# Three transformer-like blocks on one core: stage ends as written sequences, a first tile in halves, warmed matmuls, a reordered mixer

## The reference

```
# first network, layer 0 (norms 1 and 2) and layer 1 (norms 3 and 4)
x = layer_norm(alpha * x + diff_attention(x, w_qkv, ...) @ w_o)         # norm 1
x = layer_norm(alpha * x + (silu(x @ gate) * (x @ up)) @ ffn_w_out[0])  # norm 2
x = layer_norm(alpha * x + chunk_attention(x, k_band, v_band, ...) @ b_w_o)  # norm 3
x = layer_norm(alpha * x + swiglu(x, ffn_w_in[1], ffn_w_out[1]))        # norm 4
# second network
z = rmsnorm(x, pre_mix_g) @ w_in                  # splits into zu, zv, zq, zk, zv2, zg, zlr
mixed = concat(gmlp_mixer(zu, zv), gla_mixer(zq, zk, zv2, zg, zlr)) @ w_out
x = x + rmsnorm(mixed, post_mix_g)                                      # norm 5
f = relu(rmsnorm(x, pre_ff_g) @ w_ff1) ** 2 @ w_ff2
out = x + rmsnorm(f, post_ff_g)                                         # last norm
```

## Time and profile before

| | |
|---|---|
| median of 3 runs | 1797.64 us (1797.47 to 1800.77) |
| the profiled execution | 1800.18 us, span 1797.3 us |
| TensorE matmul busy | 1769.7 us (98%), 8602 instructions |
| VectorE busy | 878.4 us (49%) |
| ScalarE busy | 673.6 us (37%) |
| POOL busy | 13.1 us (1%) |
| mean granted TensorE clock | 0.996 |
| HBM read | 173.32 MB |

### The profile page before, as it was taken

The page is one execution under the profiler, slowest core; times in us unless marked ns, Lnnn a source line. Parts: engine busy times, 40 slices in busy tenths (PEclk is TensorE's granted clock), DMA queues, the critical chain, the costliest instruction groups (busy, mean ns, idle before and its releaser), DMA issues.

```text
span 1797.3 us, 21277 instructions
## 1 busy us (share of the span) xinstructions
PE 1769.7 (98%) x8602; PEld 1448.5 (81%) x8602; DVE 878.4 (49%) x1435; ACT 673.6 (37%) x1125; POOL 13.1 (1%) x39
## 2 busy tenths in 40 slices
PE   8999999999999999999999999999999999999998
PEld 6777778888888897667888888888878898888886
DVE  4688773433333634555733333339436762434353
ACT  4467623222223234655222231233444542324141
POOL 0000000000000000000000000000000000000000
PEclk9999999999999999999999999999999999999999
DMA  8232223323333343222233332353223323233321
GB/s 279 93 98 85 86 81 105 107 82 102 98 94 118 94 129 93 72 83 77 71 100 97 102 117 71 95 152 107 60 60 103 108 94 105 87 102 94 106 82 47
DMA packets 218019, 176.84 MB, mean 98 GB/s; under 512 B 8977, under 2 KB 177842, under 8 KB 217922
## 3 DMA queue, kind: packets, MB, share of 16 engines
q1 hardware_dynamic: 217922, 175.49, 32.5%
HBM read 173.32 MB, written 7.38 MB: 101 GB/s over the span
## 4 chain that ended last, share of the span: by engine, by line
PE 95%; DVE 3%; ACT 1%; issue 0%; DMA 0%; SPq 0%; ACTq 0%
PE ps L559 29%; PE ps L561 29%; PE ps L560 28%; PE ps L817 2%; PE ps L859 1%; PE ps L883 1%; PE ps L871 1%; PE ps L837 1%; PE ps L756 1%; PE ps L827 0%; DVE wlo L1314 0%; PE ps L847 0%; DVE x L1403 0%; DVE arena L1443 0%; DVE small L1407 0%
## 5 line engine op out<-in xcount | busy, mean ns | idle before, releaser
L559 PE MATMUL ps<-xh,whi 128*128 128x512 f32 (+1 forms) x1184 | 443.9, 375 | 0.2 <-DVE xl L1327 0.2
L561 PE MATMUL ps<-xh,wlo 128*128 128x512 f32 (+1 forms) x1184 | 432.6, 365 | 0.0
L560 PE MATMUL ps<-xl,whi 128*128 128x512 f32 (+1 forms) x1184 | 432.0, 365 | 0.0
L1314 DVE TENSOR_TENSOR wlo<-raw,whi 128x1024 fp32r<-128x1024 f32 x235 | 283.2, 1224 | 251.4 <-ACT whi L1018 250.7
L1018 ACT ACTIVATE whi<-raw 128x1024 fp32r<-128x1024 f32 x235 | 243.6, 1050 | 125.4 <-PE ps L561 85.0
L559 PEld LDWEIGHTS ps<-xh,whi 128*128 128x128 f32 x1184 | 223.4, 189 | 45.8 <-issue 10.5
L559 PE MATMUL ps<-whi,hh 128*128 128x512 f32 x640 | 255.1, 399 | 3.7 <-DVE hl L1540 3.7
L561 PEld LDWEIGHTS ps<-xh,wlo 128*128 128x128 f32 x1184 | 223.3, 189 | 36.4
L560 PEld LDWEIGHTS ps<-xl,whi 128*128 128x128 f32 x1184 | 223.6, 189 | 35.9 <-issue 1.4
L561 PE MATMUL ps<-whi,hl 128*128 128x512 f32 x640 | 250.4, 391 | 0.0
L560 PE MATMUL ps<-wlo,hh 128*128 128x512 f32 x640 | 250.2, 391 | 0.0
(11 more groups left out here) (197 smaller groups left out, 2026.3 us busy)
## 6 DMA issues: line engine op xcount, KB each, us to landing
raw<-in_ffn_w_in SPq DMA_DIRECT2D x88, 512.0 KB, 4.0
raw<-in_w_ff SPq DMA_DIRECT2D x64, 512.0 KB, 4.2
raw<-in_ffn_w_out SPq DMA_DIRECT2D x44, 512.0 KB, 3.8
raw<-in_a_w_qkv SPq DMA_DIRECT2D x24, 512.0 KB, 4.8
raw<-in_w_in SPq DMA_DIRECT2D x20, 512.0 KB, 3.8
raw<-in_kv_w SPq DMA_DIRECT2D x16, 512.0 KB, 4.3
bias_skewed<-bias_rows SPq DMA_DIRECT2D x8, 640.0 KB
raw<-in_a_w_o SPq DMA_DIRECT2D x8, 512.0 KB, 4.7
```

Of the source, the lines that this page charges most:

```text
L559: e.matmul(o, ah, bh, start=start, stop=False)
L560: e.matmul(o, ah, bl, start=False, stop=False)
L561: return e.matmul(o, al, bh, start=False, stop=stop)
L1314: e.tensor_tensor(lo, self.raw[:, m % RAW, :], f32(hi), ALU.subtract).then_inc(s.lo, 1)
```

## The change

It has six parts.

- Each stage end (norms 1 to 5) is a written list of words, `EDGES`. L is the next left piece in order, a0 to a3 the last left piece of a row block, b0 to b3 the next right piece of a row block. T loads the root's function table, p is one pump, n, y, f, x are `ln`, `yscale`, `feat`, `xsplit` of a row block. Behind the bar, h is the first half of the next projection, and F ends the list. Between the first word that isn't a piece and F only p pumps.
- At norm 1 the early pieces are 19 instead of 15. At norm 3 they stay 15. At norm 5 five pieces instead of three stand ahead of the squares.
- The first tile of the kernel and its blocks of x are transferred, split and multiplied in two halves each. Ahead of them TensorE does 16 matmuls of 128x128 ones, whose result nobody reads.
- In the last norm the weights are multiplied in ahead of the root, the left halves between other row blocks and the right halves beside the squares. Then one operation scales by the root and adds to x. POOL's adds go.
- The mixer's string has another order.
- The explicit table load ahead of each head's Ln goes.

```
-ORDER_MIX = "v4 C0 C1 v4 D0 v4 T0 I0 D1 v4 T1 U0 I1 g4 U1 g4 O0 g4 N0 N1 O1 g4 N2 N3 z z6 V z10"
+ORDER_MIX = "v4 C0 C1 v4 D0 v3 D1 v1 T0 I0 v3 g1 T1 v1 I1 g2 U0 g1 U1 g4 O0 g2 N0 g1 N1 g1 O1 g1 N2 g1 N3 g2 z z6 V z10"
+EDGES = {
+    1: """L L L L L L L L L L L L b0 b0 p p b0 b1 b2 b1 p b1 a0 b0 a1 b2 T p b1 n0 a2 b2 n1 b3 b2 f0 x0 a3 n2 b3
+        f1 x1 b3 p b3 f2 | x2 h n3 h h f3 F p x3 h""",
+    2: """L L L L L L L L L L L L a0 a1 a2 a3 b0 b0 b0 T p b0 n0 b1 b1 b1 b1 n1 b2 f0 x0 b2 b2 b2 b3 f1 x1 n2 b3
+        b3 b3 | h f2 x2 n3 h h f3 x3 p p h F""",
+    3: """L L L L L L L L L L L L b0 b0 b0 a0 a1 a2 a3 T p b0 n0 b1 b1 b1 b1 n1 b2 f0 x0 b2 b2 b2 b3 f1 x1 n2 b3
+        b3 b3 | h f2 x2 n3 h h f3 x3 p p h F""",
+    4: """L L L L L L L L L L L L a0 a2 b0 b0 T a1 b0 p p b0 a3 n0 b1 b1 b1 b1 y0 n1 b2 b2 b2 b2 f0 x0 b3 b3 b3 y1
+        f1 p x1 n2 b3 | h y2 n3 p y3 h f2 x2 h h f3 h x3 F""",
+    5: """L L L L L L L L b0 b0 L L L L a0 a1 a2 p p b0 b0 T n0 b1 a3 b1 b1 b1 y0 n1 b3 b2 b2 b2 b2 b3 f0 y1 b3 x0
+        f1 x1 n2 p b3 | h y2 n3 h h p f2 p y3 x2 h h f3 F x3 h""",
+}
...
             if t == 3:
                 self.done(tile, "rows", r.value)
-            if ends and first and t == 3 and norm >= 4:
-                self.feat(norm, 0)
-                self.xsplit(norm, 0)
-            elif ends and first and t >= 2 and norm < 4:
-                self.feat(norm, t - 2)
-                self.xsplit(norm, t - 2)
...
-            for _ in range(15):
+            for _ in range(ready_pieces(1)):
                 next(out)
...
-        self.some(out, 3)
+        self.some(out, 5)
...
+        w.wait_ge(s.ones, 1)
+        for _ in range(WARM):
+            e.matmul(ps[7][:, 0:128], ones[:], ones[:], start=True, stop=True)
...
+                if tile == 0:
+                    w.wait_ge(s.begin_lo, 1)
+                    w.wait_ge(s.xl, 1)
+                    a = slice(t * 128, t * 128 + 128)
+                    mm3(e, ps[b][:], xh[:, 0, a], xl[:, 0, a], wh[:, 0, :], wl[:, 0, :], True, False)
+                    begun.append(b)
+                    if t == 3:
+                        w.wait_ge(s.lo, 1)
+                        w.wait_ge(s.xl, 2)
+                        for i, b in enumerate(begun):
+                            a = slice(i * 128, i * 128 + 128)
+                            m = mm3(e, ps[b][:], xh[:, 1, a], xl[:, 1, a], wh[:, 1, :], wl[:, 1, :], False, False)
+                        m.then_inc(s.rows, 1)
+                    continue
...
             elif what == "outer_norm":
                 h, _, b = arg
-                e.preload_act_table_set(LN_EXP)
...
+                    if r.group == 3:
+                        n = nh * 4 + t
+                        if 0 < n <= 4:
+                            left = self.mb[:, n - 1, 0:512]
+                            w.wait_ge(s.g[0], 96)
+                            w.wait_ge(s.fsum, n)
+                            e.tensor_tensor(left, left, gvec[0][:, 0:512], ALU.mult).then_inc(s.gained, 1)
+                        if nh == 1:
+                            right = self.f_out[t % 2]
...
+                            e.tensor_tensor(right, self.mb[:, t, c], gvec[0][:, c], ALU.mult).then_inc(s.gained, 1)
...
-                            e.scalar_tensor_tensor(self.mb[:, t, c], self.mb[:, t, c], rs[:, t:t + 1], gvec[0][:, c],
-                                                   ALU.mult, ALU.mult).then_inc(s.scaled, 1)
-                            if half == 0 or t == 3:
-                                w.wait_ge(s.scaled, 2 * t + half + 1)
-                                e.tensor_tensor(x[:, t, c], x[:, t, c], self.mb[:, t, c], ALU.add).then_inc(s.add, 1)
+                            for half, gained in enumerate((self.mb[:, t, 0:512], right)):
+                                c = slice(half * 512, half * 512 + 512)
+                                e.scalar_tensor_tensor(x[:, t, c], gained, rs[:, t:t + 1], x[:, t, c], ALU.mult,
+                                                       ALU.add).then_inc(s.fin, 1)
...
-        for m in range(RAW):
+        _, name, at, k0, nh = self.plan.tiles[0]
+        for k, x_in, raw_in in ((0, s.begin_x, s.begin_w), (1, s.xt[0], s.raw[0])):
+            rows = slice((k0 + k) * 128, (k0 + k) * 128 + 128)
+            e.dma_start(self.xt[:, k, :], ap["c_xt"][:, k, :]).then_inc(x_in, 16)
+            e.dma_start(self.raw[:, 0, k * 512:k * 512 + 512],
+                        tables[name][rows, at + nh * 512:at + nh * 512 + 512]).then_inc(raw_in, 16)
+        for m in range(1, RAW):
```

More of the change, by code:

```diff
@@ L97, in pump @@
     def pump(self, most=2):
-        while most and self.slots and not self.waiting and self.n_split < len(self.tiles) + AHEAD:
+        while most and self.slots and self.n_split < len(self.tiles) + self.ahead:
             slot, free = self.slots.pop(0)
@@ L206, in projections, with edge @@
             self.step("half", job, 1)
             self.post(job)
-        for w in wanted[n:]:
+        for w in wanted[len(jobs):]:
             self.run(self.quarters(*w))
-    def rows(self, kind, source, row0, nk, k_first=0, hh=True, norm=None, group=0, early=False):
+    def edge(self, norm, word):
+        if word == "T":
+            self.step("table", SQRT)
+        elif word == "p":
+            self.pump(1)
+        else:
+            {"n": self.ln, "y": self.yscale, "f": self.feat, "x": self.xsplit}[word[0]](norm, int(word[1]))
@@ L218, in rows @@
         left = [(0, t, k) for k in blocks for t in range(4)]
[L219 to L224 removed]
+        if norm is None:
+            order = left + [(1, t, k) for k in blocks[:-n] for t in range(4)] + [
+                (1, t, k) for t in range(4) for k in blocks[-n:]]
+        else:
+            order = EDGES[norm][:EDGES[norm].index("|")]
+            right = {t: list(blocks) for t in range(4)}
         out, taken = {}, {}
[L226 removed]
+        for word in order:
+            if norm is None:
+                nh, t, k0 = word
+            elif word == "L":
+                nh, t, k0 = left.pop(0)
+            elif word[0] == "a":
+                nh, t, k0 = 0, int(word[1]), blocks[-1]
+            elif word[0] == "b":
+                nh, t = 1, int(word[1])
+                k0 = right[t].pop(0)
+            else:
+                self.by_hand, self.ahead = True, SPLIT + EXTRA
+                self.edge(norm, word)
+                continue
             first, last = k0 == blocks[0], k0 == blocks[-1]
[L228 removed]
             if first:
[L230 to L238 removed]
+                out[nh, t] = Rows(kind, nh, t, self.bank(hold=True), None, norm, group)
             if t == 0:
@@ L242, in rows @@
             signal = last or t == 3
+            if last:
+                r.i = self.count(kind)
             ready = max(self.h[k0], self.h[k0 + 1]) if hh else None
@@ L314, in attention_a @@
         self.step("prepare_a")
-        out = self.rows("res", ("a_w_o", 0), 0, 8, norm=1, early=True)
+        out = self.rows("res", ("a_w_o", 0), 0, 8, norm=1)
         def proj(h):
@@ L411, in fill @@
                 yield from proj(p)
[L412 removed]
+            for _ in range(ready_pieces(3)):
                 next(out)
```

174 lines of the change are left out of this document (79 added, 95 removed).

## The result

The changed kernel takes 1788.69 us (median of five runs, 1788.55 to 1790.53) against 1797.64 (five runs, 1797.47 to 1800.77): 8.95 us less, a ratio of 0.9948 with a 95% interval of 0.9934 to 0.9963. The prediction was 1786.5 in a range of 1781 to 1791.5, and "faster" with 0.94. The profiled execution took 1788.67 us, with a span of 1786.9.

A forecast was written before the change was run, and what follows sets the result against it. TensorE, busy 1769.7 of 1797.3 us, was the bound, with only waits and half clock to win. Terms 3.1 + 0 + 0 + 1.3 + 0.1 + 4.7 + 1.9 = 11.1 took 1800.18 to 1789.1, median 1786.5 (2.5 lower); range 1781 to 1791.5.

The forecast's parts named there:

- The start: First tiles: TensorE starts near 6.1, tile 1 at 12.2 instead of 15.37; 3.1 us gained.
- The bound given for it: At the start: the low bound on the gain, 1.5 us, if the 256 KB transfers land later.
- rival (c): At the start: the matmuls on ones do nothing; 0.9 us less gain, 1787.4, inside the forecast, no separate chance.
- The last head and norm 1: Last head to norm 1: 4.6 plus 0.7 us gained, 5.7 paid at busy VectorE; taken as 0, ends -0.4 and +5.3.
- The new wait behind the ones-matmul: Last head: the next piece must wait for the ones-matmul's bank until ScalarE has read it, 0.8 us.
- The three gaps: Norm 1: TensorE idles 4.0 us waiting for VectorE, in parts of about 2.2, 1.0 and 0.8.
- Rival (a): Norm 1: VectorE keeps up as waits and costs overlap more; 5.3 us more gain, about 1780.6; chance 0.22.
- Norms 2 and 3: Norms 2 and 3: order as before, nothing gained; norm 3's wait and half clock stay; bounds -1 and +1.
- Norm 4: Norm 4: a half projection behind f3 hides the 1.6 us xl wait, about 0.3 taken back; gain 1.3.
- The mixer: Mixer: waits at U0 and O1 go, with the clock loss behind U0; gain 4.7 us, bounds 2 and 4.8.
- The tail: Behind the last matmul: two fused passes save 1.45 us, lateness 0.5; gain 1.9, bounds 1.2 and 2.2.
- The term for the stores: Tail: the last two stores, 0.7 us apart, may disturb each other by 0.1 us.

The follow-up runs named there:

- light norm 1: Changed kernel with norm 1's weights g and b left out, one VectorE pass per half instead of two, for timing only: 1783.52 us.
- old norm 1: Changed kernel with only the end of norm 1 set back to 15 early pieces and the old order: 1790.88 us.
- the other order: Changed kernel with norm 1's written order altered: x1 split ahead of n2, a half projection ahead of block 2's transposes, one pump moved: 1788.34 us.
- no warming: Changed kernel without the 16 matmuls on ones at the start: 1791.6 us.
- x whole: Changed kernel with the x of tile 0 in one transfer of 512 KB, its weights still in two halves: 1789.06 us.
- old start: Changed kernel with the whole start as before: no matmuls on ones, tile 0 and its x in one piece each: 1791.95 us.
- old tail: Changed kernel with only the last norm set back: root, scaling by root and weights, addition, three right halves added by POOL: 1792.55 us.
- combined: Changed kernel with tile 0's x in one 512 KB transfer and norm 1's x1 split ahead of n2: 1784.65 us, 0.992 of the kernel before.
- old mixer: Changed kernel with the mixer's old order string, still without explicit table loads: 1793.09 us.
- explicit loads: Changed kernel with the explicit Ln and Exp table load ahead of each head's Ln put back: 1788.14 us.
- more pumps: Changed kernel with two pumps moved into norm 3's early pieces; VectorE's order stayed the same: 1788.94 us.
- old norm 4: Changed kernel with only norm 4's written order set back, halves needing x3 directly behind f3: 1790.26 us.

## Why the prediction came out as it did

**What bounds the kernel** was read rightly. TensorE's work is fixed, and every gain and loss was a wait, a stretch of half clock or the two ends.

**The start (3.1 predicted, 1.27 measured) is the term that was mis-sized.** That tile 0's start does not decide, and tile 1's xl does, held. The failed step is that the transfers of tile 1 land when they did before, because the queue is full anyway. They landed at 10.50, where ScalarE had taken them up at 8.75 before, issued 0.9 later and transported at a rate that fell to 225 GB/s. The later issue was to be foreseen: SP starts its first transfers 0.44 to 0.51 us apart in both traces, whether they have 256 or 512 KB, and tile 0 now takes four of them instead of two (the prediction speaks of eight small ones). The bound given for it, 1.5 for late landings, was not wide enough. Two smaller steps were wrong as well: the ones don't end in time (they cost tile 0 1.28), and the first real matmul came at 7.26, not near 6.1. Both are hidden by the same wait. So rival (c), the warming does nothing, came true at tile 1, where its 0.9 doesn't count.

**The last head and norm 1 (0 predicted, -0.41 measured)** were right by place and cause, and by size as far as the clock lets one tell. The new wait behind the ones-matmul was to be 0.8 and is 0.78. The three gaps were to be 2.2, 1.0 and 0.8 and are 2.28, 0.82 and 0.33, and the clock fell behind them (5 us at 0.66, 1.7). The light norm 1 shows that VectorE is the cause, the old norm 1 that the added pieces only move the waiting. It puts them at +0.3, the ledger at -0.4. The difference has a cause: the old norm 1 in the changed kernel lost 3.4 of clock behind its 3.7 and the kernel before 1.7, while only the kernel before waited 0.67 for f0. That makes 1.0 where 0.7 is to be explained; the rest is not assigned. Rival (a), VectorE keeps up, is out (its own terms add up to 1780.2, not 1780.6). I called it VectorE's load; the other order shows that 2.0 of the 5.1 was not load but order, as n2's passes stand in front of the split that TensorE needs first. I had not looked for that.

**Norms 2 and 3 (0 predicted).** The waits at norm 3 are as they were. That the half clock stays with them was wrong for this execution: it didn't fall. It is no gain of the change, as the kernels derived from it show it in some traces and not in others.

**Norm 4 (1.3 predicted, 1.82 measured)** had the right cause; the 0.3 that I let the weight split and y3 take back was not taken. **The mixer (4.7 predicted, 4.55 measured)** held; 3.0 of it is in the waits, the rest depends on the clock. That the table loads are hidden held. The count was to be five to seven and is seven. By the Trainium skill (ScalarE: Activation LUTs, What ACT_TABLE_LOAD costs) a switch is about 2.66 us with the draining; the traces show the 1.28 of the load alone, with the next operation 0.02 behind it. **The tail (1.9 predicted, 1.54 measured)**: 1.45 and 0.5 were right to 0.02. The term for the stores, 0.1, was 0.4. The fixed cost of about 2 us that the prediction takes from the Trainium skill (DMA: Bandwidth & Descriptors, Anatomy of one DMA) is given there for transfers that GpSimd issues; these are SP's, and from the last pass to the end of the span the traces have 2.4 before and 2.8 after.

**The sum and the median.** The profiled execution was to come to 1789.1 and came to 1788.67, which looks exact and is luck in two places: 1.8 too much at the start was made up by 1.6 of clock at norm 3, and the span, still 0.7 longer than predicted, by 1.1 less around it. The median, predicted by the same difference of 2.5 as before, is 2.2 higher than predicted. The profile of before was of an execution with the half clock at norm 3 and 2.9 us around the span, that of after had no half clock there and 1.8 around. Over all their runs the kernel before has 1.7 to 3.0 around its span, the changed kernel 1.7 to 1.8, so up to some 1.1 us of a difference of totals lies outside the spans, and no experiment here says why. A difference of two medians must not be worked out from the difference of one profile to its median; this is the second step that failed.

**Still open.** Why the clock falls behind norm 3's waits in some executions. What slows the transport at the start when x comes in two transfers. And whether fewer matmuls on ones would win part of the 0.9 that they hold up tile 0 when x comes whole (6.91 against 6.05); that wasn't tried.

## What to carry to other kernels

Before early work is laid under a wait, look at how busy the engine is that works behind it: where VectorE has 24.6 of 26 us to do, TensorE only arrives earlier at the next wait, and what then helps is less work there, or that work in the order in which it is needed. A first tile in halves is worth what the second tile's landing allows, so look at that landing after every change of the first transfers. And compare stages between two traces by the start of the same matmul, since a stretch of half clock that comes and goes, at 1.7 us or at 3.4, is larger than most single edits.

## What the runs showed of the hardware that was not expected

- **The clock behind equal waits.** All 14 traces have two waits at norm 3, of 0.97 to 1.00 and 0.88 to 0.89 us. In seven of them (before, no warming, x whole, old start, norm 1's other order, old tail, combined) the granted clock fell behind them, with a mean of 0.89 from 857 to 872; in the other seven (changed, light norm 1, old mixer, explicit loads, more pumps, old norm 4, old norm 1) it stayed at 1.00, the 2.4 GHz level. Behind the three waits of norm 1 it fell in all nine traces that have them, for 3.4 us in six and for 6.8 us in three (no warming, old mixer, old tail): 1.7 or 3.4 lost behind the same waits. The 3.70 for hl brought it down both times, for 3.4 us before and 6.8 with the old norm 1. A wait of 1.74 us at norm 1 did so once in two traces, and one of 1.57 us once in four: in the mixer of the kernel before, but not in the mixer with the old string, nor at norm 4 before or set back. Waits of 0.68 to 1.79 us for tile 1's xl didn't bring it down, 2.02 did. Here about one to two microseconds of waiting is a region in which either can happen, at a price of 1.7 when it does.
- **A transfer split in two can slow its followers.** With x as one transfer of 512 KB instead of two of 256, tile 1's weights landed at 8.95 (two traces) instead of 10.07 to 10.85 (ten traces). In each of the ten the rate falls to 225 GB/s or less between 4.5 and 7 us; in the four with x in one piece it stays above 330 from 3.5 to 8 us.
- **Small fp32 matmuls in a row.** 16 of 128x128 stand as 32 records and took 5.8 to 6.6 us from 1.07 in eleven traces, longer than the wait that they were to fill. They start 0.21 us apart, and 0.11 once the clock is up, which comes at 5.1 to 6.9 us; without them it is up at 9.2.
